# A transformer and mixture-of-experts layer on one core: the first stage transposes x before its norm is known, and the sigmoids move to ScalarE

## The reference, cut to what matters

```python
def rms_norm(x, g):
    xf = x.astype(jnp.float32)
    return (xf * lax.rsqrt(jnp.mean(xf * xf, axis=-1, keepdims=True) + EPS) * g).astype(x.dtype)
...
def gdn_mixer(qkv, z, b, a, conv_w, a_log, dt_bias, norm_g):
    B, T, _ = qkv.shape
    qkv = jax.nn.silu(causal_conv(qkv, conv_w))
...
    o = gated_delta_rule(q, k, v, beta, g)
    o = rms_norm(o, norm_g) * jax.nn.silu(heads(z).astype(jnp.float32))
```

## Time and profile before

| | |
|---|---|
| Time, median of 3 runs | 1031.4 us (1031.37 to 1032.32) |
| Profiled execution | span 1029.0 us from first to last instruction; its own time is not recorded apart from the span |
| PE, share of the span | 973.9 us (95%) |
| DVE | 437.0 us (42%) |
| ACT | 182.1 us (18%) |
| Mean DMA rate | 293 GB/s of HBM traffic |

### The profile page before, as it was taken

How to read it: one execution, slowest core, us unless ns; L and a number is a source line. 1 busy time by engine, 2 the same in 40 slices (tenths; PEclk the granted TensorE clock), 3 DMA queues, 4 the chain that set the end, 5 groups by cost and what they waited for, 6 DMA issues and landing times.

```text
span 1029.0 us, 15519 instructions
## 1 busy us (share of the span) xinstructions
PE 973.9 (95%) x6439; PEld 545.2 (53%) x6439; DVE 437.0 (42%) x811; ACT 182.1 (18%) x419; POOL 28.7 (3%) x88
## 2 busy tenths in 40 slices
PE   7999999999999999999999899999889988888996
PEld 6788876576666665558774533333233332322332
DVE  3868377274555557402223562722213222222213
ACT  2233334210000000203442101110011011000111
POOL 8100000000000000000000000000000000000000
PEclk9999998999999999999999999999999999999999
DMA  8424022484766689561343899999999999999994
GB/s 351 177 97 157 3 82 82 153 359 188 286 283 282 286 342 421 216 267 39 125 161 109 323 402 423 426 427 429 425 427 426 425 427 429 426 427 427 417 413 192
DMA packets 30097, 302.49 MB, mean 294 GB/s; under 512 B 5968, under 2 KB 6096, under 8 KB 11472
## 3 DMA queue, kind: packets, MB, share of 16 engines
q1 hardware_dynamic: 30032, 301.53, 71.6%
HBM read 300.47 MB, written 1.05 MB: 293 GB/s over the span
## 4 chain that ended last, share of the span: by engine, by line
PE 69%; DMA 21%; SPq 6%; DVE 2%; ACT 1%; issue 1%; DVEq 0%; ACTq 0%
PE PS L1640 11%; PE PS L1244 10%; PE PS L1239 9%; PE PS L1689 8%; PE PS L1986 7%; DMA slot<-in_moe_w_up_dram 7%; SPq L671 5%; PE PS L2005 5%; DMA slot<-in_moe_w_gate_dram 4%; DMA XH<-in_moe_w_gate_dram 4%; DMA XH<-in_moe_w_up_dram 4%; PE PS L1469 2%; PE PS L1587 2%; PE PS L1962 2%; DMA slot<-in_moe_w_down_dram 2%; PE PS L1937 1%
## 5 line engine op out<-in xcount | busy, mean ns | idle before, releaser
L1640 PE MATMUL PS<-XH,slot 128*128 128x256 f32 x512 | 113.3, 380 | 1.7 <-DVE XH L2510 0.9
L1640 PEld LDWEIGHTS PS<-XH,slot 128*128 128x128 f32 x512 | 97.2, 190 | 21.2 <-issue 8.9
L1239 PE MATMUL PS<-XH,slot 128*128 128x256 f32 x432 | 97.6, 383 | 0.0
L1239 PEld LDWEIGHTS PS<-XH,slot 128*128 128x128 f32 x432 | 80.8, 190 | 12.3 <-issue 1.2
L2005 PE MATMUL PS<-slot,ATT 128*32 128x512 f32 x576 | 67.1, 619 | 10.7 <-DMA slot<-in_moe_w_up_dram 10.7
L1986 PE MATMUL PS<-slot,ATT 128*32 128x512 f32 x544 | 65.4, 607 | 7.8 <-issue 4.1
L1244 PE MATMUL PS<-slot,XH 128*128 128x256 f32 (+4 forms) x224 | 71.7, 476 | 0.0
L1986 PE MATMUL PS<-slot,MASKS 128*32 128x512 f32 x576 | 64.3, 594 | 1.4 <-DMA slot<-in_moe_w_down_dram 0.8
L2559 DVE SCALAR_TENSOR_TENSOR AR<-AR 128x384 f32<-128x384 f32 (+1 forms) x112 | 59.9, 611 | 0.0
L1962 PE MATMUL PS<-AR,DIAG 128*128 128x512 f32 x120 | 57.6, 606 | 0.0
L1244 PEld LDWEIGHTS PS<-slot,XH 128*128 128x128 f32 x224 | 42.0, 190 | 26.1 <-issue 14.8
(11 more groups left out here) (467 smaller groups left out, 1194.4 us busy)
## 6 DMA issues: line engine op xcount, KB each, us to landing
slot<-in_moe_w_up_dram SPq DMA_DIRECT2D x18, 2048.0 KB, 30.5
slot<-in_w_ffn_dram SPq DMA_DIRECT2D x16, 2048.0 KB, 8.3
slot<-in_moe_w_gate_dram SPq DMA_DIRECT2D x16, 2048.0 KB, 36.5
slot<-in_moe_w_down_dram SPq DMA_DIRECT2D x16, 2048.0 KB, 36.5
AR<-in_ada_w_dram SPq DMA_DIRECT2D x16, 1536.0 KB, 14.7
AR<-in_moe_w_gate_dram SPq DMA_DIRECT2D x9, 2048.0 KB, 34.0
AR<-in_moe_w_down_dram SPq DMA_DIRECT2D x8, 2048.0 KB, 36.5
AR<-in_moe_w_up_dram SPq DMA_DIRECT2D x8, 2048.0 KB, 35.0
```

The costliest lines, as they stand in the source:

```text
L1239: ins = pe.matmul(dst, w[:, c * width + col:c * width + col + n], HT[:, c, :], start=(c == 0), stop=(c == KC - 1))
L1640: ins = pe.matmul(PS[:, b, (f % 2) * T:(f % 2 + 1) * T], slots[s][:, c * 512 + f * P:c * 512 + (f + 1) * P], HT[:, c, :], start=(c == 0), ...
```

## The change

1. PE transposes x itself against the identity (`first_transposes`), without waiting for the norm; ahead of that it runs 8 matmuls of the identity with itself into a bank that is overwritten later. The banks `norm0_0` to `norm0_2` are emptied by DVE, `norm0_3` by ACT, with the gain alone.
2. The roots go on when projections are emptied. For tokens on partitions, ACT's copy takes `scale=RSTD[:, i]`. For channels on partitions, one matmul of ones with both `DIAG` tiles (`root_rows`, after block 0 of qkv) puts the roots in rows, ACT copies them to `ROOTS`, and DVE multiplies: `take_channels` moves to DVE, and `kcvc` is multiplied in place in PSUM by DVE before ACT's pieces.
3. `in0` comes as four transfers of 512 KB, one for each block.
4. The sigmoids of the convolution and of z: ACT does exp(-c), then Ln(1 + e), then exp(-l), each waiting for the one before; DVE only multiplies.
5. Several semaphores are merged into one counted twice; the order of the waits stays.

```diff
-    g = [(f"norm0_{b}", "DA"[b % 2]) for b in range(4)]
+    g = [(f"norm0_{b}", "DDDA"[b]) for b in range(4)] + [("root_rows", "A")]
...
-    g += [(f"qkv{b}", "A") for b in range(3)] + [("bq0", "A"), ("bq1", "A"), ("kw0", "A")]
+    g += [(f"qkv{b}", "D") for b in range(3)] + [("bq0", "A"), ("bq1", "A"), ("kw0", "A")]
...
-    g += [("gc", "D")] + [(f"r{b}", "A") for b in range(3)] + [("qkv4", "A"), ("kw1", "A")] + [(f"qk{b}", "A") for b in range(3)]
-    g += [("kv0", "A")] + [(f"kk{b}", "D") for b in range(6)] + [("qkv3", "A")]
+    g += [("gc", "D")] + [(f"r{b}", "A") for b in range(3)] + [("qkv4", "D"), ("kw1", "A")] + [(f"qk{b}", "A") for b in range(3)]
+    g += [("kv0", "A")] + [(f"kk{b}", "D") for b in range(6)] + [("qkv3", "D")]
...
+            for j in range(4):
+                sp.dma_start(slots[0][:, j * D:(j + 1) * D], a["w_in"][in_at:in_at + P * D].rearrange("(p n) -> p n", p=P))\
+                    .then_inc(sems[f"in0_column{j}" if j < 3 else "loaded0"], 16)
+                in_at += P * D
...
-                    step(act.activation(HT[:, 4 * i:4 * i + 4, :].rearrange("p (h c) t -> p h (c t)", h=2),
+                    step(act.activation(CV[:, 4 * i:4 * i + 4, :].rearrange("p (h c) t -> p h (c t)", h=2),
                                         XR[:, i, :].rearrange("p (h d) -> p h d", h=2), ACT.Square, accum_out=SS[:, i:i + 1]))
+                    if i == 1:
+                        bank_ = wait_filled(act, "norm0_3")
+                        act.wait_ge(sems["cols_loaded"], 16)
+                        for c in (6, 7):
+                            ins = act.activation(HT[:, c, :], bank_[:, (c % 2) * T:(c % 2 + 1) * T], ACT.Copy, scale=COL[:, R_MIX + c:R_MIX + c + 1])
+                        ins.then_inc(sems["emptied_by_act"], 1)
                     rsqrt(RSTD[:, i:i + 1], SS[:, i:i + 1], 1.0 / D, LNV[:, i:i + 1], sems["rstd_ready"])
-                for b in (1, 3):
-                    bank_ = wait_filled(act, f"norm0_{b}")
-                    if b == 1:
-                        act.wait_ge(sems["cols_loaded"], 16)
-                    for c in (2 * b, 2 * b + 1):
-                        ins = act.activation(HT[:, c, :], bank_[:, (c % 2) * T:(c % 2 + 1) * T], ACT.Copy, scale=COL[:, R_MIX + c:R_MIX + c + 1])
-                    ins.then_inc(sems["emptied_by_act"], 1)
...
-                    ins = act.activation(dst, src(b), ACT.Copy)
+                    ins = act.activation(dst, src(b), ACT.Copy, scale=scale)
...
-                act.activation(EX[:, 2 * b:2 * b + n, :], CV[:, 2 * b:2 * b + n, :], ACT.Exp, scale=-1.0)\
-                    .then_inc(sems["conv_exp"], 1)
-
-            def take_channels(b):
-                n = 2 if b < 4 else 1
-                empty(f"qkv{b}", (QKVT[:, 2 * b:2 * b + n, 3:3 + T], lambda s: s[:, 0:n * T].rearrange("p (j t) -> p j t", t=T)))
-
-            take_channels(0)
-            take_channels(1)
+                ex = EX[:, 2 * b:2 * b + n, :]
+                step(act.activation(ex, CV[:, 2 * b:2 * b + n, :], ACT.Exp, scale=-1.0))
+                step(act.activation(ex, ex, ACT.Ln, bias=EPSC[:, 1:2]))
+                act.activation(ex, ex, ACT.Exp, scale=-1.0).then_inc(sems["conv_exp"], 1)
+
+            root = lambda i: RSTD[:, i:i + 1]
+            empty("root_rows", (ROOTS, lambda s: s[:, 0:T]))
             silu_exp(0)
             silu_exp(1)
-            take_channels(2)
             silu_exp(2)
             act.wait_ge(sems["const_ready"], 3)
...
+            act.wait_ge(sems["kcvc_scaled"], 1)
             empty("kcvc", *parts)
             take_selected(1)
             silu_exp(3)
...
-                empty(f"z{i}", (SIG[:, i, 0:GW], lambda s: s[:, 0:GW]))
+                empty(f"z{i}", (SIG[:, i, 0:GW], lambda s: s[:, 0:GW]), scale=root(i))
                 wait_emptied(act, f"z{i}")
-                act.activation(SG[:, i, 0:GW], SIG[:, i, 0:GW], ACT.Exp, scale=-1.0).then_inc(sems["sig_exp"], 1)
+                z = SG[:, i, 0:GW]
+                step(act.activation(z, SIG[:, i, 0:GW], ACT.Exp, scale=-1.0))
+                step(act.activation(z, z, ACT.Ln, bias=EPSC[:, 1:2]))
+                act.activation(z, z, ACT.Exp, scale=-1.0).then_inc(sems["sig_exp"], 1)
...
-            def norm_transposes():
+            def first_transposes():
+                pe.wait_ge(sems["const_ready"], 1)
+                for k in range(8):
+                    pe.matmul(bank("norm0_3")[:, 0:P], IDENT[:, :], IDENT[:, :], start=True, stop=True)
                 for i in range(NT):
-                    pe.wait_ge(sems["xn_ready"], i + 1)
+                    pe.wait_ge(sems[f"x_loaded{i}"], 16)
                     for b4 in range(4):
                         if i == 0:
                             pe_open(pe, f"norm0_{b4}")
                         for c in (2 * b4, 2 * b4 + 1):
                             o = (c % 2) * T + i * P
-                            ins = pe.matmul(bank(f"norm0_{b4}")[:, o:o + P], XR[:, i, c * P:(c + 1) * P], DIAG[:, i, :], start=True, stop=True)
+                            ins = pe.transpose(bank(f"norm0_{b4}")[:, o:o + P], XR[:, i, c * P:(c + 1) * P], IDENT[:, :])
                         if i == NT - 1:
                             ins.then_inc(filled, 1)
 
-            norm_transposes()
+            def root_rows():
+
+                pe.wait_ge(sems["const_ready"], 2)
+                pe.wait_ge(sems["xn_ready"], NT)
+                b = pe_open(pe, "root_rows")
+                pe.matmul(b[:, 0:T], ONES[:, :], DIAG[:, :, :].rearrange("p a b -> p (a b)"), start=True, stop=True).then_inc(filled, 1)
+
+            first_transposes()
...
-                    w = weights(f"in{j // 4}")
-                    ins = channel_major(b[:, (j % 2) * T:(j % 2) * T + T], w, 512, (j % 4) * P, first=(j == 0))
+                    dst = b[:, (j % 2) * T:(j % 2) * T + T]
+                    if j < 4:
+                        if j < 3:
+                            pe.wait_ge(sems[f"in0_column{j}"], 16)
+                            w = slots[0]
+                        else:
+                            w = weights("in0")
+                        ins = channel_major(dst, w[:, j * D:(j + 1) * D], P, 0, first=(j == 0))
+                        if j == 0:
+                            root_rows()
+                    else:
+                        ins = channel_major(dst, weights(f"in{j // 4}"), 512, (j % 4) * P)
...
+                dve.wait_ge(sems["cols_loaded"], 16)
+                for b4 in range(3):
+                    b = wait_filled(dve, f"norm0_{b4}")
+                    for c in (2 * b4, 2 * b4 + 1):
+                        ins = ts(HT[:, c, :], b[:, (c % 2) * T:(c % 2 + 1) * T], gain[:, c:c + 1], None, ALU.mult)
+                    ins.then_inc(freed, 1)
                 dve.wait_ge(sems["const_ready"], 1)
                 for i in range(NT):
                     dve.wait_ge(sems["rstd_ready"], i + 1)
                     ts(DIAG[:, i, :], IDENT[:, :], RSTD[:, i:i + 1], None, ALU.mult).then_inc(sems["xn_ready"], 1)
-                dve.wait_ge(sems["cols_loaded"], 16)
-                for b4 in (0, 2):
-                    b = wait_filled(dve, f"norm0_{b4}")
-                    for c in (2 * b4, 2 * b4 + 1):
-                        ins = ts(HT[:, c, :], b[:, (c % 2) * T:(c % 2 + 1) * T], gain[:, c:c + 1], None, ALU.mult)
-                    ins.then_inc(freed, 1)
...
+            def take_channels(g):
+                n = 2 if g < 4 else 1
+                b = wait_filled(dve, f"qkv{g}")
+                tt(QKVT[:, 2 * g:2 * g + n, 3:3 + T], b[:, 0:n * T].rearrange("p (j t) -> p j t", t=T), bc(ROOTS, 1, n), ALU.mult)\
+                    .then_inc(freed, 1)
...
-                step(ts(EX[:, js, :], EX[:, js, :], 1.0, None, ALU.add))
-                step(dve.reciprocal(EX[:, js, :], EX[:, js, :]))
                 tt(CV[:, js, :], CV[:, js, :], EX[:, js, :], ALU.mult).then_inc(sems["silu_ready"], 1)
 
+            wait_emptied(dve, "root_rows")
+            take_channels(0)
             convolve(0)
+            take_channels(1)
             convolve(1)
             silu(0)
+            take_channels(2)
             convolve(2)
             silu(1)
             silu(2)
...
             step(ins)
+            take_channels(4)
             convolve(4)
...
-                z = SG[:, i, 0:GW]
-                step(ts(z, z, 1.0, None, ALU.add))
-                step(dve.reciprocal(z, z))
-                tt(SIG[:, i, 0:GW], SIG[:, i, 0:GW], z, ALU.mult).then_inc(sems["z_gated"], 1)
+                tt(SIG[:, i, 0:GW], SIG[:, i, 0:GW], SG[:, i, 0:GW], ALU.mult).then_inc(sems["z_gated"], 1)
 
             dve.wait_ge(sems["const_ready"], 6)
+            take_channels(3)
             level(0)
+            b = wait_filled(dve, "kcvc")
+            for kv in range(2):
+                ins = tt(b[:, kv * T:(kv + 1) * T], b[:, kv * T:(kv + 1) * T], ROOTS, ALU.mult)
+            ins.then_inc(sems["kcvc_scaled"], 1)
```

(19 more changed lines are left out.)

49 lines of the change are left out of this document (23 added, 26 removed).

## The result

The kernel before has a median of 1031.4 us, the changed one 1034.5 us (1031.3 to 1038.4, 9 runs). The ratio is 1.0030, with a 95% interval of 1.0016 to 1.0044: slower by 1.7 to 4.5 us. A second timing on another occasion gave 1034.9 us and 1.0041 (1.0029 to 1.0053). The profiled execution of the changed kernel took 1034.8 us, with a span of 1032.9 us against 1029.0.

What follows compares the result with a forecast made beforehand. PE was taken to set the pace until the expert weight stream, so early shifts carry through. Terms -4.8 + 0.4 + 0.1 + 4.1 + 1.7 + 1.0 = +2.5 us on 1031.4 gave 1033.9 us; own range 1032.7 to 1035.2.

Steps and rivals of the forecast that it cites:

- The start: First qkv blocks: PE starts them at 7.9 us instead of 12.7, -4.8 us (bounds -5.1 and -4.0).
- Root rows: After qkv block 0: one added matmul of 256 columns, two passes, costs +0.4 us.
- Groups 0 to 2 and qk: Up to kv0: DVE's relief buys nothing; ACT's longer group 4 chain delays the kw1 and qk copies, +0.1 us.
- Level 1: Before P2: DVE's wait for kcvc makes convolve(3) and ACT's copies late; PE stands still, +4.1 us (3.6 to 4.6).
- The clock behind it: After the level 1 standstill: 3.4 us at half speed, +1.7 us (bounds 0 and 2.5).
- z0: Level 6, before solve(0): z0's added Ln and exp stand ahead of the TT60 and TT61 copies, +1.0 us (0.6 to 1.3).
- The shift carried to the end one for one: Whole kernel: PE sets the pace until the expert weight stream, so an early shift reaches the end in full.
- The dip at 154 to 161 us: Around mixed(0, 0): low clock costing some 3.0 us, taken to stay; rival that it does not come, 1030.9 us, chance 0.12.
- the one of a head start at low clock: Rival, start: PE's rate does not rise or falls back, transposes and first blocks slow, +2.9 us, 1036.8 us; chance 0.20.
- level 1 was not cheap: Rival, level 1: copies of T and TT not held up, head start kept, -3.3 us, 1028.1 us; chance 0.08.
- the clock did fall: Rival, after the level 1 standstill: the clock stays up, total +0.8 us, 1032.2 us; chance 0.15.

Runs made afterwards that it cites:

- the kernel before with the passes alone: The kernel before with only the sigmoids of the convolution and z changed to Exp, Ln, Exp on ACT: 1033.1 us, ratio 1.0022.
- both orders and the old sigmoids: Changed kernel with DVE's and ACT's level 1 work reordered around kcvc, and sigmoids as before the change: 1030.6 us, ratio 0.9987.
- The orders: Changed kernel, convolve(3) and work before it ahead of DVE's kcvc multiply: 1029.3 us; also silu_exp(3) ahead of ACT's kcvc pieces: 1028.7 us.
- the filler: Changed kernel with 16 identity matmuls added on PE in the standstill before P2: 1033.9 and 1031.6 us, ratios 1.0030 and 1.0008.
- the split: Changed kernel with DVE and ACT reordered at level 1, z0's passes moved behind the copies solve(0) needs: 1027.5 and 1027.6 us.
- both orders: Changed kernel with convolve(3) ahead of the kcvc multiply on DVE and silu_exp(3) ahead of the kcvc pieces on ACT: 1028.7 us, ratio 0.9978.
- the old sigmoids: Changed kernel with the sigmoids as before: one Exp on ACT; add, reciprocal and multiply on DVE: 1033.6 us, ratio 1.0031.

## Why the prediction was right, and where its terms were off

The forecast was 1033.9 us, with a range of its own of 1032.7 to 1035.2; measured were 1034.5 and 1034.9 us. By its steps, each in the profile of the changed kernel:

- **The start, -4.8: too large by about 0.8.** The mechanism was right: transposes end, DVE empties `norm0_0` and the first block lands, all near the same time. Two sizes were off. The sum lets the rate of TensorE rise 3.7 us after it begins, so that the 16 transposes run at 0.116 us a pass. In this profile it rose later: the first ten took 2.15 us, so the bank was out at 8.50 instead of 7.6. And the first block landed 6.2 us after its issue at 2.2, at 8.4 instead of 7.9. PE began at 8.63, and the first block took 3.69 us instead of 3.46. The rise differs from execution to execution: in the ten profiles of kernels with this start the 16 transposes took 1.91 to 3.17 us, and in seven of them it was the first block of the weights, not DVE, that came last. PE began between 8.04 and 8.87 us. With the root rows the token projections came 3.57 us early, where the sum had 4.8 - 0.4 = 4.4.
- **Root rows, +0.4:** 0.43 us.
- **Groups 0 to 2 and qk, +0.1: the sign was wrong.** PE gained 0.22 us here (3.79 - 3.57). The step said DVE's relief buys nothing, since before silu(2) ends 0.2 us ahead of its need and PE doesn't wait. But the first weight load of the transposes did wait for it in the trace of before:

```profile
47.79 1.29 PEld L1269 LDWEIGHTS PS<-IDENT,AR 128*128 128x128 f32 x12 [0.29 <-DVE AR L2260]
```

In the kernel before with the passes alone this wait is gone, and the transposes are done 0.2 us sooner after the token projections. The cover came as forecast: silu(2) ends at 36.98 us, which with the 3.79 us is 7.0 us ahead of before. What the step did not say is that the relief is needed for the head start: PE comes 3.6 us earlier now, and the run with both orders and the old sigmoids shows the 0.70 us that it would have waited.
- **Level 1, +4.1:** 4.10 us. Step by step, with PE's 3.79 us of head start added to the times of the new trace: convolve(3) ends at 88.85 + 3.79 = 92.64, forecast 92.65; ACT's copies begin at 90.83 + 3.79 = 94.62, forecast 94.6. The orders showed that it is DVE's wait for `kcvc` ahead of work that needs nothing from it.
- **The clock behind it, +1.7:** it fell, as after the standstill in the earlier trace rows, and P2 and hid0 took (2.83 - 1.48) + (4.54 - 3.61) = 2.3 us more than before. Of this 0.2 us is not the clock: right after a wait P2 takes 1.67 us at the full clock too, as with the filler. That leaves 2.1 us here, 1.5 and 1.2 us in two other profiles. The term took a low stretch of 3.4 us from another stage; here it lasted from 89.6 to 96.5 us, and PE worked in the last 4.8 us of it.
- **z0, +1.0:** 0.90 us, shown by the split.
- **The shift carried to the end one for one:** it held. The shift is 3.54 us at 188 us, 3.54 us at the 32 passes of L1962 (L1937 of before; 605.05 against 601.51 us), and 3.9 us in the span.
- **The dip at 154 to 161 us:** it came again, for 7 us, as in the earlier trace rows. The estimate that it costs some 3.0 us agrees with the one profile without it (46.2 against 49.2 us).

The sum of the measured terms is -3.57 - 0.22 + 4.10 + 2.28 + 0.90 = +3.5 us, and the profile shows +3.5 us from `solve(0)` to mixed(0, 0) and on. The forecast had +2.5. Of the difference 0.8 us is the start, 0.6 us the clock, and -0.4 the small terms.

Of the rivals, the one of a head start at low clock asked for a rate that does not rise because of the transposes. Its first half came in part: the transposes took 3.17 us in the profile of the changed kernel, nearer to its 3.7 than to the sum's 1.9. The second half, blocks at half speed for 3.6 us, did not come, and in the profile with both orders the transposes too ran at the full rate (16 in 1.91 us). The run without extra matmuls speaks against the reason: PE did nothing but transposes until 8.3, and the blocks had their full rate from 10 us on. The Trainium skill, "TensorE: Matmul & The Clock Gate", Part 4: PE-mode transpose, says that transposes do not count as busy as matmuls do. The 16 transposes here did not hold the rate down beyond the first block; what they add towards its rise, against the block's own passes from 8.68 on, this run doesn't separate. Of the other rivals, level 1 was not cheap and the clock did fall; the low clock near 155 us stayed away in one of 14 profiles, and not in that of the changed kernel.

That the total came within 1 us has a little luck in it: the start was 0.8 us worse than its term and what followed the standstill 0.6 us, and the small terms, 0.4 us better, took part of that back.

What stays open: why the clock is low between 150 and 170 us for 0 to 17 us, and how much of the 3 us between the medians with the passes on ACT and with the old sigmoids, both orders mended, is more than the 1.3 us that the profiles show.

## What to carry to other kernels

An instruction that waits for a late bank belongs behind everything on its engine that does not need it. Here the same instructions in another order were worth 6 us, more than the whole change of the first stage. A head start must be followed engine by engine to its end: what had 0.2 us of slack for the old arrival is late for the new one, and moving work to another engine may be worth nothing until then. Added dependent passes go behind the copies that the bounding engine waits for, even if it takes splitting a helper in two.

## What the runs showed of the hardware

- The granted clock fell to 0.50 in the standstills of 4.10 us at level 1 (in the second profile of the changed kernel 0.3 us after its end) and of 4.58 us ahead of the first block with `in0` whole, and after the one of 1.98 us with the old sigmoids; with 0.47 and 1.13 us it did not. One wait of 2.11 us, ahead of the first block in the first profile of the filler, left no mark either: the block took 3.72 us, against 3.62 for a block later. Sixteen matmuls that compute nothing kept the clock at 1.00 in the standstill (both profiles). It fell as well where PE was busy nearly without a gap: in the kernel with both orders at 151.7 us, with PE at 0.94 of each of the two microseconds up to 152 us.
- In the first microseconds the column of the granted clock reads 1.00 while passes take twice as long as later: in the changed kernel the 16 passes of the identity from 1.58 us on took 3.78 us, 0.24 us each, and 24 of the same shape from 46.24 us on 2.78 us, 0.116 us each, all at 1.00. There the rate of passes has to be read, not the clock.
- ACT's Ln with a tile as bias took 0.72 us for 128x512, Exp with a constant scale 0.63 us; for 128x384 0.61 and 0.52 us.
